# Residual added on VectorE, norms in SBUF, a shared column multiplication and six output buffers in the combine stage of a two-layer mixture-of-experts trunk

## The chip, the cores and the metric

The kernel runs on one core of a Trainium2 chip. The metric is the device time in microseconds (us) of one execution, as the median of several. The program's engines are TensorE (PE, its weight loads PEld), VectorE (DVE), ScalarE (ACT), GpSimd (POOL) and SyncE (SP, which here only issues transfers).

## The reference

Two layers work on 1024 tokens of 1024 columns, all in float32. Each layer has a mixer and then a mixture of experts, in which every token goes to two experts. This is what ends a layer; the change touches nothing else:

```python
y = hierarchical_moe(h, ...)                      # for each token: w0 * expert row 0 + w1 * expert row 1
x = layer_norm(DEEPNORM_ALPHA * x + (1.0 + gt_f) * y, ln_ffn_g[layer], ln_ffn_b[layer])
# layer_norm: (x - mean) * rsqrt(var + eps) * g + b, over the 1024 columns of a token
```

## The kernel before

The program is a row of stages, each with an instruction list of its own for every engine, written out by hand; the lists of a stage start when the engines have left the stage before. The experts' stage writes two scaled rows for each token to memory (`y_dram`). The last stage of each layer, `combine`, then brings them together. It is the stage that changes, and it runs twice: with the tag `f0c` after layer 0's experts (some 1545 to 1617 us of the span) and with `f1c` after layer 1's (3273 to the end).

`combine` works on eight tiles of 128 tokens, t = 0 to 7. For a tile SP loads the two sets of expert rows (`r0`, `r1`) and the residual `x`, 512 KB each, in four buffers. TensorE forms the sum in PSUM (`py`, three buffers): in each half of 512 columns two matmuls with a diagonal matrix of the tokens' weights (L2759) and one with ALPHA times the identity on `x` (L2760), each recorded as two passes. VectorE takes mean and variance from PSUM (`bn_stats` L2782, `bn_aggr` L2784), and adds epsilon (L2786). ScalarE takes the root (L2809), VectorE the reciprocal (L2791) and `nmr` = -mean * rstd (L2793), both of one column. ScalarE normalizes from PSUM into `z` in SBUF (L2817, four buffers), VectorE multiplies by the gain row (L2800), GpSimd adds the bias row (L2827) and issues the store (L2829).

VectorE's list is a loop over n in which three tiles are under way: statistics of tile n, then reciprocal and `nmr` of tile n-1, then the gain of tile n-2. In `f0c` the next layer's input is prepared as well: TensorE transposes each finished tile (L322, after the bias of that tile), and ScalarE (L328) and VectorE (L335) bring the halves to SBUF with a scale and a shift; VectorE does that for tile n-3 at the end of round n. In `f0c` SP also issues the first loads of the next stage's weights (`ret_w`) behind its last `x`.

The waits that matter: TensorE waits for all three loads of a tile and, from tile 3, for the normalization of tile t-3. The gain waits for ScalarE's normalization, the bias for the gain, and the store for the bias. `f1c` ends with the last store, `f0c` with the last tile's L335.

Of the kernel before, what the change touches and what calls it, by code (L numbers as in the profile page):

```python
# [17 lines left out]
P = 128  # L18
D = 1024
# [2693 lines left out]
def combine(g, tag, r, y_dram, x_dram, out_dram, layer, ahead=None):  # L2713
    nc, io = g.nc, g.io
    NR, NB = 4, 3
    with ExitStack() as ctx:  # L2716
# [11 lines left out]
        names = "vec_in weighed summed stat moments rooted rstdd nmrd normed gained done".split()  # L2728
        S = dict(zip(names, g.sems(ctx, tag, *names)))
        r_in = g.sems(ctx, tag, *[f"r_in{b}" for b in range(NR)])  # L2730
        stored = g.sems(ctx, tag, *[f"stored{b}" for b in range(NR)])
        block = g.stage(ctx)

        @block.sync
        def _(sp):
            for t in range(NT):
                if t >= NR:
                    sp.wait_ge(S["summed"], t - NR + 1)
                for k in range(2):
                    sp.dma_start(rows[k][t % NR][:, :], y_dram[k * T + t * P:k * T + (t + 1) * P, :])\  # L2740
                        .then_inc(r_in[t % NR], 16)
                sp.dma_start(x[t % NR][:, :], x_dram[t * P:(t + 1) * P, :]).then_inc(r_in[t % NR], 16)
                if t == 1:
                    sp.dma_start(gain_b[:, :], io["ln_ffn_g"][layer].partition_broadcast(P)).then_inc(S["vec_in"], 16)
                    sp.dma_start(bias_b[:, :], io["ln_ffn_b"][layer].partition_broadcast(P)).then_inc(S["vec_in"], 16)
            if ahead:
                ahead.first_loads(sp)

        @block.tensor
        def _(pe):  # L2750
            pe.wait_ge(S["weighed"], 2 * NT + 1)
# [53 lines left out]
        def _(act):  # L2805
            for n in range(NT + 3):
# [121 lines left out]
```

## Time and profile before

| what | value |
|---|---|
| median of 3 executions | 3352.03 us (3344.8, 3352.03, 3352.76) |
| the profiled execution's own time | 3342.8 us |
| its span, first to last instruction | 3341.1 us |
| TensorE busy | 3009.4 us, 90% of the span |
| VectorE / ScalarE / GpSimd busy | 1211.8 / 879.7 / 582.9 us |
| stage `f0c`, first VectorE instruction to last | 1545.66 to 1616.32 us |
| stage `f1c`, first VectorE instruction to the last store's issue | 3273.30 to 3336.74 us |
| memory traffic in the span | 606.22 MB read, 45.40 MB written |

Times of the table's lower part are microseconds from the span's start. The share of busy time is an average over all stages, and the two combine stages are some 72 and 68 us of 3341; so they are to be read for themselves. The profiled execution is 9 us below the median of the others.

### The profile page before, as it was taken

To read this page: it belongs to the slowest core of one execution; us is meant where nothing else is said; L and a number is where in the kernel's file an instruction comes from. 1 tells how busy PE (TensorE), PEld (TensorE's weight loads), DVE (VectorE), ACT (ScalarE), POOL (GpSimd) and SP (SyncE) were. 2 spreads that over 40 slices of the span, in tenths; PEclk is the share of its full clock that TensorE was granted. 3 is DMA by queue.
4 is the path that set the end of the run, shared out by engine and by line. 5 is a ranking of instruction groups with operands and counts; after the bars stand their busy time and mean duration, and the time that the engine had idled before them with its cause. 6 is when DMAs were issued, how large, how long until landed. Compare 5 with 4: busy or idle time off the path is not lost. (4 is left out here: it accounts for less than half of the span.)

```text
span 3341.1 us, 45315 instructions
## 1 busy us (share of the span) xinstructions
PE 3009.4 (90%) x16595; PEld 1617.1 (48%) x16596; DVE 1211.8 (36%) x3016; ACT 879.7 (26%) x1770; POOL 582.9 (17%) x1031
## 2 busy tenths in 40 slices
PE   8969999698969999998899999999899969988886
PEld 6546544485434443333566666666544434433332
DVE  5867844473442122223333223322312231221224
ACT  1034334142121111111354445544501111111111
POOL 0000010471111222212211111111200011221213
PEclk9979999698979999999899999999999979999998
DMA  8910011233168999996311101110041088999985
GB/s 328 351 55 1 1 29 48 62 75 106 66 261 338 401 419 417 414 404 234 129 38 38 33 6 39 38 38 1 1 147 38 32 350 349 375 423 410 420 359 217
DMA packets 181866, 625.66 MB, mean 187 GB/s; under 512 B 53795, under 2 KB 104754, under 8 KB 147670
## 3 DMA queue, kind: packets, MB, share of 16 engines
q1 hardware_dynamic: 152150, 579.05, 44.4%
q0 software_dynamic: 20576, 42.01, 3.3%
q10 hardware_dynamic: 8992, 2.62, 0.3%
q8 instruction: 93, 1.52, 0.2%
q14 instruction: 55, 0.45, 0.0%
HBM read 606.22 MB, written 45.40 MB: 195 GB/s over the span
## 5 line engine op out<-in xcount | busy, mean ns | idle before, releaser
L1977 PE MATMUL ret_pqkv<-ret_w,hT_mix 128*128 128x512 f32 x1024 | 452.4, 595 | 1.9 <-PEq L2716 1.9
L1839 PE MATMUL mo_py<-mo_w,mixT 128*128 128x512 f32 x768 | 336.2, 598 | 4.8 <-DMA mo_w<-in_ret_w_out_dram 2.5
L2530 PE MATMUL f1e_pgu<-f1w_gu,f1e_xT 128*64 128x512 f32 x1056 | 253.3, 635 | 65.6 <-DMA f1w_gu<-in_moe_w_up_dram 53.5
L1977 PEld LDWEIGHTS ret_pqkv<-ret_w,hT_mix 128*128 128x128 f32 x1024 | 190.5, 191 | 218.0 <-issue 218.0
L2530 PE MATMUL f0e_pgu<-f0w_gu,f0e_xT 128*64 128x512 f32 x1056 | 247.9, 624 | 32.5 <-DMA f0w_gu<-in_moe_w_up_dram 15.0
L1839 PEld LDWEIGHTS mo_py<-mo_w,mixT 128*128 128x128 f32 x768 | 146.4, 192 | 187.4 <-issue 179.5
L1985 PE MATMUL ret_pgate<-ret_w,hT_mix 128*128 128x256 f32 x1024 | 231.6, 379 | 0.0
L1985 PEld LDWEIGHTS ret_pgate<-ret_w,hT_mix 128*128 128x128 f32 x1024 | 189.6, 190 | 23.6 <-issue 0.5
L2530 PEld LDWEIGHTS f1e_pgu<-f1w_gu,f1e_xT 128*64 128x64 f32 x1056 | 82.9, 146 | 228.3 <-issue 171.9
L2127 DVE TENSOR_TENSOR ret_state<-ret_state,ret_pout 128x256 f32<-128x256 f32 x56 | 23.6, 421 | 441.3 <-PE ret_pout L2009 441.3
L2530 PEld LDWEIGHTS f0e_pgu<-f0w_gu,f0e_xT 128*64 128x64 f32 x1056 | 82.8, 144 | 187.6 <-issue 168.6
L478 PE MATMUL gc_pq<-hT_mix,gc_w 128*128 128x512 f32 x384 | 168.3, 597 | 0.7 <-PEq L861 0.7
L1963 POOL TENSOR_TENSOR ret_z<-ret_z,ret_gain 128x256 f32<-128x256 f32 x64 | 46.5, 726 | 653.2 <-DVE ret_z L2138 653.2
L2680 DVE COPY f1e_hidT<-f1e_ph 128x384 f32<-128x384 f32 x33 | 18.4, 558 | 336.8 <-PE f1e_ph L2554 336.7
L2680 DVE COPY f0e_hidT<-f0e_ph 128x384 f32<-128x384 f32 x33 | 18.4, 558 | 331.6 <-PE f0e_ph L2554 331.6
L2562 PE MATMUL f1e_pd<-f1w_d,f1e_hidT 128*64 128x512 f32 x528 | 120.6, 598 | 1.1 <-DVE f1e_hidT L2680 1.1
L2562 PE MATMUL f0e_pd<-f0w_d,f0e_hidT 128*64 128x512 f32 x528 | 120.6, 598 | 0.9 <-DVE f0e_hidT L2680 0.9
L2641 ACT ACTIVATE f1e_hs<-f1e_pgu 128x256 f32<-128x256 f32 x33 | 12.7, 384 | 411.2 <-PE f1e_pgu L2530 411.2
L2048 ACT COPY ret_v<-ret_pqkv 128x256 f32<-128x256 f32 x64 | 23.8, 373 | 368.0 <-PE ret_pqkv L1977 368.0
L478 PEld LDWEIGHTS gc_pq<-hT_mix,gc_w 128*128 128x128 f32 x384 | 73.4, 192 | 92.9 <-issue 92.9
L2641 ACT ACTIVATE f0e_hs<-f0e_pgu 128x256 f32<-128x256 f32 x33 | 12.7, 384 | 384.0 <-PE f0e_pgu L2530 384.0
L1699 DVE TENSOR_TENSOR mo_z<-mo_py,mo_gate_b 128x1024 f32<-128x1024 f32 x16 | 19.6, 1225 | 238.2 <-PE mo_py L1839 238.2
(591 smaller groups left out, 4719.4 us busy)
## 6 DMA issues: line engine op xcount, KB each, us to landing
f0w_gu<-in_moe_w_gate_dram SPq DMA_DIRECT2D x33, 2048.0 KB, 18.4
f0w_gu<-in_moe_w_up_dram SPq DMA_DIRECT2D x33, 2048.0 KB, 26.4
f0w_d<-in_moe_w_down_dram SPq DMA_DIRECT2D x66, 1024.0 KB, 19.5
f1w_gu<-in_moe_w_gate_dram SPq DMA_DIRECT2D x33, 2048.0 KB, 20.0
f1w_gu<-in_moe_w_up_dram SPq DMA_DIRECT2D x33, 2048.0 KB, 30.8
f1w_d<-in_moe_w_down_dram SPq DMA_DIRECT2D x66, 1024.0 KB, 22.0
mixT<-in_ada_w_dram SPq DMA_DIRECT2D x80, 512.0 KB, 5.9
ret_w<-in_ret_w_in_dram SPq DMA_DIRECT2D x16, 1024.0 KB, 10.0
```

What stands on the lines that cost most here:

```text
L478: mm = pe.matmul(pq[u][:, half * 512:(half + 1) * 512], w[u][:, kk, :], g.hT[:, kk, half * 512:(half + 1) * 512], start=(kk == 0), stop=(k ...
L1699: dve.tensor_tensor(z[:, :], y, self.gate_b[:, :], ALU.mult).then_inc(S["zmul"], 1)
L1839: mm = pe.matmul(py[t % 3][:, half * 512:(half + 1) * 512], mixT[:, kk, t * P:(t + 1) * P], ws[:, kk, half * 512:(half + 1) * 512], start= ...
L1963: pool.tensor_tensor(zb, zb, gain[:, h, :], ALU.mult).then_inc(S["gained"], 1)
L1977: mm = pe.matmul(p_qkv[s % 2][:, :], g.hT[:, kk, t * P:(t + 1) * P], w[h % 2][:, kk, 0:512], start=(kk == 0), stop=(kk == KD - 1))
L1985: mm = pe.matmul(p_gate[s % 2][:, 0:RDV], g.hT[:, kk, t * P:(t + 1) * P], w[h % 2][:, kk, 512:W], start=(kk == 0), stop=(kk == KD - 1))
L2048: act.copy(v[b][:, :], p_qkv[s % 2][:, QK:512])
L2127: ch.mark(dve.tensor_tensor(st[:, :], state[(s - 1) % 2][:, :], p_out[:, RDV:2 * RDV], ALU.add))
L2530: mm = pe.matmul(pgu[0][h * LOW:(h + 1) * LOW, :], xT[u][:, kk, 0:LOW], ew.gu[u][:, :, kk, h * FH:(h + 1) * FH], start=(kk == 0), stop=(kk ...
L2562: mm = pe.matmul(pd[0][h * LOW:(h + 1) * LOW, :], hidT_low[:, k % 2, k // 2, :], ew.d[u][:, k, h * DH:(h + 1) * DH], start=(k == 0), stop= ...
L2641: act.activation(hs[0][:, :], pgu[0][:, 0:FH], ACT.Silu).then_inc(S["silu_a"], 1)
L2680: dve.tensor_copy(hidT[:, :], ph[:, 0:4 * CAP]).then_inc(S["hTd"], 1)
```

## The change

TensorE no longer adds the residual: the matmuls with ALPHA times the identity go. VectorE adds ALPHA * x as it takes the sum from PSUM into `z`, and statistics, normalization, gain and bias all work in SBUF. A PSUM buffer is free once VectorE has taken the sum, and TensorE waits for two of the weight matrices and for the expert rows only. `x` has semaphores of its own. The gain is split: VectorE multiplies columns 0 to 511, GpSimd columns 512 to 1023, and then GpSimd adds the bias to all. On VectorE the gain now stands ahead of the reciprocal and `nmr` in a round. `z` has six buffers.

```diff
-    NR, NB = 4, 3
+    NR, NB, NZ = 4, 3, 6
+    HD = D // 2
...
-                sp.dma_start(x[t % NR][:, :], x_dram[t * P:(t + 1) * P, :]).then_inc(r_in[t % NR], 16)
+                if t >= NR:
+                    sp.wait_ge(S["residual"], t - NR + 1)
+                sp.dma_start(x[t % NR][:, :], x_dram[t * P:(t + 1) * P, :]).then_inc(x_in[t % NR], 16)
...
-            pe.wait_ge(S["weighed"], 2 * NT + 1)
             for t in range(NT):
-                pe.wait_ge(r_in[t % NR], 48 * (t // NR + 1))
+                pe.wait_ge(S["weighed"], 2 * t + 2)
+                pe.wait_ge(r_in[t % NR], 32 * (t // NR + 1))
                 if t >= NB:
-                    pe.wait_ge(S["normed"], t - NB + 1)
+                    pe.wait_ge(S["residual"], t - NB + 1)
...
-                        pe.matmul(py[t % NB][:, cols], weights[:, t, k, :], rows[k][t % NR][:, cols], start=(k == 0), stop=False)
-                    mm = pe.matmul(py[t % NB][:, cols], alpha[:, :], x[t % NR][:, cols], start=False, stop=True)
+                        mm = pe.matmul(py[t % NB][:, cols], weights[:, t, k, :], rows[k][t % NR][:, cols], start=(k == 0),
+                                       stop=(k == 1))
...
                     dve.wait_ge(S["summed"], t + 1)
+                    dve.wait_ge(x_in[t % NR], 16 * (t // NR + 1))
...
+                    dve.scalar_tensor_tensor(out=zt[:, :], in0=x[t % NR][:, :], scalar=ALPHA, in1=py[t % NB][:, :],
+                                             op0=ALU.mult, op1=ALU.add).then_inc(S["residual"], 1)
+                    dve.wait_ge(S["residual"], t + 1)
                     for half in range(2):
-                        dve.bn_stats(stats[:, t, half, :], py[t % NB][:, half * 512:(half + 1) * 512]).then_inc(S["stat"], 1)
+                        dve.bn_stats(stats[:, t, half, :], zt[:, half * HD:(half + 1) * HD]).then_inc(S["stat"], 1)
...
+                if 0 <= n - 2 < NT:
+                    t = n - 2
+                    if t == 0:
+                        dve.wait_ge(S["vec_in"], 32)
+                    dve.wait_ge(S["normed"], t + 1)
+                    dve.tensor_tensor(z[t % NZ][:, 0:HD], z[t % NZ][:, 0:HD], gain_b[:, 0:HD], ALU.mult).then_inc(S["gained_a"], 1)
                 if 0 <= n - 1 < NT:
...
-                if 0 <= n - 2 < NT:
-                    t = n - 2
-                    if t == 0:
-                        dve.wait_ge(S["vec_in"], 32)
-                    dve.wait_ge(S["normed"], t + 1)
-                    dve.tensor_tensor(z[t % NR][:, :], z[t % NR][:, :], gain_b[:, :], ALU.mult).then_inc(S["gained"], 1)
...
-                    act.activation(z[t % NR][:, :], py[t % NB][:, :], ACT.Identity, bias=nmr[:, t:t + 1],
+                    act.activation(z[t % NZ][:, :], z[t % NZ][:, :], ACT.Identity, bias=nmr[:, t:t + 1],
...
-                pool.wait_ge(S["gained"], t + 1)
-                pool.tensor_tensor(z[t % NR][:, :], z[t % NR][:, :], bias_b[:, :], ALU.add).then_inc(S["done"], 1)
+                zt = z[t % NZ]
+                pool.wait_ge(S["normed"], t + 1)
+                pool.tensor_tensor(zt[:, HD:D], zt[:, HD:D], gain_b[:, HD:D], ALU.mult).then_inc(S["gained_b"], 1)
+                pool.wait_ge(S["gained_a"], t + 1)
+                pool.wait_ge(S["gained_b"], t + 1)
+                pool.tensor_tensor(zt[:, :], zt[:, :], bias_b[:, :], ALU.add).then_inc(S["done"], 1)
```

The first place is VectorE's list in `f1c`, the round of tile 4 and the start of the next. A number behind `py`, `z` or `x` is that of the buffer. Before, the round is:

```order
L2782 BN_STATS f1c_stats<-f1c_py1 128x6 x2
L2784 BN_AGGR f1c_mv<-f1c_stats 128x2
L2786 TENSOR_SCALAR f1c_rstd<-f1c_mv 128x1
L2791 RECIPROCAL f1c_rstd<-f1c_rstd 128x1
L2793 SCALAR_TENSOR_TENSOR f1c_nmr<-f1c_mv,f1c_rstd 128x1
L2800 TENSOR_TENSOR f1c_z2<-f1c_z2,f1c_gain_b 128x1024
L2782 BN_STATS f1c_stats<-f1c_py2 128x6 x2
```

With the change it is:

```order
L2788 SCALAR_TENSOR_TENSOR f1c_z4<-f1c_x0,f1c_py1 128x1024
L2792 BN_STATS f1c_stats<-f1c_z4 128x6 x2
L2794 BN_AGGR f1c_mv<-f1c_stats 128x2
L2796 TENSOR_SCALAR f1c_rstd<-f1c_mv 128x1
L2802 TENSOR_TENSOR f1c_z2<-f1c_z2,f1c_gain_b 128x512
L2807 RECIPROCAL f1c_rstd<-f1c_rstd 128x1
L2809 SCALAR_TENSOR_TENSOR f1c_nmr<-f1c_mv,f1c_rstd 128x1
L2788 SCALAR_TENSOR_TENSOR f1c_z5<-f1c_x1,f1c_py2 128x1024
```

A multiplication-and-addition of 1024 columns has come ahead of the statistics, which now read `z`. The gain is half as wide, and it has moved from behind `nmr` to ahead of the reciprocal: behind the gain came the next tile's statistics, and now come the reciprocal and `nmr` of one column.

The second place is GpSimd's list in `f1c`, about tiles 3 to 5 before:

```order
L2827 TENSOR_TENSOR f1c_z3<-f1c_z3,f1c_bias_b 128x1024
L2829 DMA out_0_dram<-f1c_z3 128x1024
L2827 TENSOR_TENSOR f1c_z0<-f1c_z0,f1c_bias_b 128x1024
L2829 DMA out_0_dram<-f1c_z0 128x1024
L2827 TENSOR_TENSOR f1c_z1<-f1c_z1,f1c_bias_b 128x1024
```

and about tiles 2 and 3 with the change:

```order
L2834 TENSOR_TENSOR f1c_z2<-f1c_z2,f1c_gain_b 128x512
L2837 TENSOR_TENSOR f1c_z2<-f1c_z2,f1c_bias_b 128x1024
L2839 DMA out_0_dram<-f1c_z2 128x1024
L2834 TENSOR_TENSOR f1c_z3<-f1c_z3,f1c_gain_b 128x512
L2837 TENSOR_TENSOR f1c_z3<-f1c_z3,f1c_bias_b 128x1024
```

For each tile a multiplication of 512 columns has come ahead of the addition.

## Rows read from the trace of the kernel before

**Rows 1.** The chain that ended last, one step (start, us, what).

```profile
3320.65 1.72 PE f1c_py L2759 x4
```

**Rows 2.** Timeline of one `f1c` tile (start, us, engine, line, operation, shapes, idle before).

```profile
3307.81 1.29 DVE L2782 BATCH_NORM_STATS2 f1c_stats<-f1c_py 128x6 f32<-128x512 f32 x2 [2.02 <-PE f1c_py L2760]
...
3309.39 0.15 DVE L2786 TENSOR_SCALAR f1c_rstd<-f1c_mv 128x1 f32<-128x1 f32 x1
...
3309.72 1.22 DVE L2800 TENSOR_TENSOR f1c_z<-f1c_z,f1c_gain_b 128x1024 f32<-128x1024 f32 x1
...
3309.84 1.21 ACT L2817 ACTIVATE f1c_z<-f1c_py,f1c_nmr,f1c_rstd 128x1024 f32<-128x1024 f32 x1
...
3311.03 2.34 POOL L2827 TENSOR_TENSOR f1c_z<-f1c_z,f1c_bias_b 128x1024 f32<-128x1024 f32 x1 [1.92 <-DVE f1c_z L2800]
...
3313.67 0.57 POOL L2829 DMA_DIRECT2D out_dram<-f1c_z  x1 [0.30 <-POOL f1c_z L2827]
```

**Rows 3.** Timeline of the end of `f1c`.

```profile
3325.17 1.22 DVE L2800 TENSOR_TENSOR f1c_z<-f1c_z,f1c_gain_b 128x1024 f32<-128x1024 f32 x1
...
3326.31 0.15 DVE L2791 RECIPROCAL f1c_rstd<-f1c_rstd 128x1 f32<-128x1 f32 x1
...
3326.48 2.33 POOL L2827 TENSOR_TENSOR f1c_z<-f1c_z,f1c_bias_b 128x1024 f32<-128x1024 f32 x1 [1.95 <-DVE f1c_z L2800]
...
3326.50 2.33 DVE L2793 SCALAR_TENSOR_TENSOR f1c_nmr<-f1c_mv,f1c_rstd 128x1 f32<-128x1 f32 x1
...
3328.75 4.71 DVE L2800 TENSOR_TENSOR f1c_z<-f1c_z,f1c_gain_b 128x1024 f32<-128x1024 f32 x2
...
3336.18 0.56 POOL L2829 DMA_DIRECT2D out_dram<-f1c_z  x1 [0.30 <-POOL f1c_z L2827]
```

**Rows 4.** Timeline of `f0c`, four places.

```profile
1570.20 1.30 DVE L2782 BATCH_NORM_STATS2 f0c_stats<-f0c_py 128x6 f32<-128x512 f32 x2 [3.15 <-PE f0c_py L2760]
...
1600.05 1.04 PE L322 MATMUL f0ct_pt<-ident,f0c_z 128*128 128x128 f32 x8
...
1604.58 0.15 DVE L2791 RECIPROCAL f0c_rstd<-f0c_rstd 128x1 f32<-128x1 f32 x1
...
1614.95 1.37 DVE L335 TENSOR_SCALAR hT_mix<-f0ct_pt,mod 128x128 f32<-128x128 f32 x4 [2.14 <-PE f0ct_pt L322]
```

**Rows 5.** Groups of instructions kept apart by shape (total us, mean ns, idle before).

```profile
L1699 DVE TENSOR_TENSOR mo_z<-mo_py,mo_gate_b 128x1024 f32<-128x1024 f32 x16 | 19.6, 1225 | 238.2 <-PE mo_py L1839 238.2
...
L1492 DVE TENSOR_TENSOR dr_Td<-dr_Td,dr_b 128x512 f32<-128x512 f32 x16 | 10.9, 679 | 4.3 <-PE dr_b L1250 4.3
...
L458 POOL TENSOR_TENSOR gdn_gate<-gdn_gate,gc_onorm 128x512 f32<-128x512 f32 x8 | 9.9, 1263 | 2.7 <-DMA gc_onorm<-in_gdn_norm_dram 2.7
```

**Rows 6.** Timeline, VectorE and GpSimd at once, two places.

```profile
697.74 0.21 POOL L1201 TENSOR_TENSOR dr_X<-dr_X,dr_outer 64x15 f32<-64x15 f32 x1
...
697.75 0.68 DVE L1542 TENSOR_REDUCE dr_oss<-dr_y 128x8 f32<-128x512 f32 x1
...
1652.20 0.73 POOL L1963 TENSOR_TENSOR ret_z<-ret_z,ret_gain 128x256 f32<-128x256 f32 x1 [33.41 <-DVE ret_z L2138]
...
1652.25 0.29 DVE L2119 TENSOR_TENSOR ret_scores<-ret_pscores,upto 128x128 f32<-128x128 f32 x1 [0.20 <-PE ret_pscores L1999]
```

**Rows 7.** The third tile's expert rows, `f1c`, then `f0c`: issues and landing.

```profile
L2740 SPq DMA_DIRECT2D f1c_r<-expert_rows x2: 486/532/579, 3277.2 to 3277.8; - x2
...
DMA to landing us min/median/max: 10.4/10.8/11.2
...
L2740 SPq DMA_DIRECT2D f0c_r<-expert_rows x2: 433/436/438, 1550.5 to 1550.9; - x2
...
DMA to landing us min/median/max: 9.9/10.3/10.7
```

**Rows 8.** Windows with TensorE partly idle (window, us, busy by engine, clock, DMA).

```profile
214.00:235.00 21.00, 16.26 (x46) 8.03 (x44) 18.99 (x78) 2.35 (x4) 0.00 (x0) 1.00 0.00 0
...
2410.00:2434.00 24.00, 12.14 (x22) 6.08 (x23) 4.40 (x16) 7.28 (x12) 4.35 (x6) 0.50 0.41 159
```

More of the change, by code:

```diff
@@ L2720, in combine @@
         rows = [[sb(f"r{k}_{b}", [P, D]) for b in range(NR)] for k in range(2)]
-        z = [sb(f"z{b}", [P, D]) for b in range(NR)]
+        z = [sb(f"z{b}", [P, D]) for b in range(NZ)]
         weights = sb("weights", [P, NT, 2, P])
-        alpha = sb("alpha", [P, P])
         stats = sb("stats", [P, NT, 2, 6])
@@ L2727, in combine @@
         turn = Turn(g, ctx, f"{tag}t", layer + 1, 0) if ahead else None
-        names = "vec_in weighed summed stat moments rooted rstdd nmrd normed gained done".split()
+        names = "vec_in weighed summed residual stat moments rooted rstdd nmrd normed gained_a gained_b done".split()
         S = dict(zip(names, g.sems(ctx, tag, *names)))
         r_in = g.sems(ctx, tag, *[f"r_in{b}" for b in range(NR)])
-        stored = g.sems(ctx, tag, *[f"stored{b}" for b in range(NR)])
+        x_in = g.sems(ctx, tag, *[f"x_in{b}" for b in range(NR)])
+        stored = g.sems(ctx, tag, *[f"stored{b}" for b in range(NZ)])
         block = g.stage(ctx)
@@ L2763, in _ @@
                     pe.wait_ge(S["done"], t - 2)
-                    turn.tensor(pe, t - 3, z[(t - 3) % NR])
+                    turn.tensor(pe, t - 3, z[(t - 3) % NZ])
             if turn:
@@ L2767, in _ @@
                     pe.wait_ge(S["done"], t + 1)
-                    turn.tensor(pe, t, z[t % NR])
+                    turn.tensor(pe, t, z[t % NZ])
         @block.vector
         def _(dve):
-            dve.tensor_scalar(alpha[:, :], g.ident[:, :], ALPHA, None, ALU.mult).then_inc(S["weighed"], 1)
             for t in range(NT):
@@ L2778, in _ @@
                 if n < NT:
-                    t = n
+                    t, zt = n, z[n % NZ]
                     dve.wait_ge(S["summed"], t + 1)
+                    dve.wait_ge(x_in[t % NR], 16 * (t // NR + 1))
+                    if t >= NZ:
+                        dve.wait_ge(stored[t % NZ], 16 * (t // NZ))
+                        if turn:
+                            dve.wait_ge(turn.turned, 2 * (t - NZ + 1))
+                    dve.scalar_tensor_tensor(out=zt[:, :], in0=x[t % NR][:, :], scalar=ALPHA, in1=py[t % NB][:, :],
+                                             op0=ALU.mult, op1=ALU.add).then_inc(S["residual"], 1)
+                    dve.wait_ge(S["residual"], t + 1)
                     for half in range(2):
-                        dve.bn_stats(stats[:, t, half, :], py[t % NB][:, half * 512:(half + 1) * 512]).then_inc(S["stat"], 1)
+                        dve.bn_stats(stats[:, t, half, :], zt[:, half * HD:(half + 1) * HD]).then_inc(S["stat"], 1)
                     dve.wait_ge(S["stat"], 2 * t + 2)
@@ L2825, in _ @@
             for t in range(NT):
-                pool.wait_ge(S["gained"], t + 1)
-                pool.tensor_tensor(z[t % NR][:, :], z[t % NR][:, :], bias_b[:, :], ALU.add).then_inc(S["done"], 1)
+                zt = z[t % NZ]
[4 more added lines that the diff above has]
+                pool.tensor_tensor(zt[:, :], zt[:, :], bias_b[:, :], ALU.add).then_inc(S["done"], 1)
                 pool.wait_ge(S["done"], t + 1)
-                pool.dma_start(out_dram[t * P:(t + 1) * P, :], z[t % NR][:, :]).then_inc(stored[t % NR], 16)
-            for b in range(NR):
-                pool.wait_ge(stored[b], 16 * (NT // NR))
+                pool.dma_start(out_dram[t * P:(t + 1) * P, :], zt[:, :]).then_inc(stored[t % NZ], 16)
+            for b in range(NZ):
+                pool.wait_ge(stored[b], 16 * ((NT - 1 - b) // NZ + 1))
 def moe(g, tag, x_dram, out_dram, layer, logits, router, following=None):
```

6 lines of the change are left out of this document (1 added, 5 removed).

## The prediction

> **What bounds the kernel now.** I read the chain of waits first. In the last stage it runs through TensorE's matmuls from tile to tile; one half of a tile's expert rows is four passes in 1.72 us, so 0.43 us each [rows 1]. A tile has 12 passes before, 5.16 us. The timeline of one tile confirms it: VectorE sat idle for 2.02 us until TensorE's last pass, started the statistics at 3307.81 and was through with the gain at 3310.94 [rows 2]. So `f1c` goes by TensorE up to its last tile; behind that VectorE, ScalarE and GpSimd follow one another, and the last store is issued at 3336.18 [rows 3]. `f0c` is the same with transposes: TensorE needs 5.16 and the eight transposes, recorded as 1.04 with the last one's end, so some 6.0 us a tile, the statistics of tile 2 start at 1570.20, VectorE's list reaches the reciprocal of tile 7 at 1604.58, and its last L335 ends at 1616.32 [rows 4]. Elsewhere nothing is edited. The change can only be worth what these two stages, 140 us, give or take.
>
> The second thing to see is at the end of `f1c`. The gain of tile 5 ends at 3325.17 + 1.22 = 3326.39. GpSimd's bias addition starts 0.09 later, at 3326.48. VectorE's `nmr`, one column wide, starts at 3326.50 and takes 2.33 us, to 3328.83, while the bias addition ends at 3328.81 [rows 3]. So a VectorE instruction with two inputs in SBUF stands still while GpSimd's addition runs. Two instructions elsewhere ran free: one with an input in PSUM took 0.29 us inside a GpSimd multiplication of 0.73, and a reduction of 512 columns from one input in SBUF took 0.68 though a GpSimd operation of 0.21 had begun 0.01 before it [rows 6]; 0.68 is what two-input instructions of that width take alone [rows 5]. Before, this costs little: in the running stage the gain is followed by statistics out of PSUM, and `nmr` comes 3.6 us later.
>
> **The change part by part.** Counted from a round's start on VectorE (the residual of tile n):
>
> *Residual.* New, 1024 columns, one input in PSUM: 1.225 us, the nearest group with such inputs and width [rows 5], and 0.03 to the next. By its inputs it doesn't meet GpSimd [rows 6].
>
> *Statistics to epsilon.* From the first `bn_stats` to the epsilon instruction 3309.39 - 3307.81 = 1.58, and an instruction that waits for nothing starts some 0.07 later [rows 2]. I take the same from SBUF. No row has `bn_stats` on SBUF beside GpSimd; bounds are 0 and a full hold (a rival below). I take 0: of the rows, the one-input reduction from SBUF is nearest, and it wasn't held [rows 6]. That it is the second input which makes an instruction wait is a reading, not shown.
>
> *Half a gain, moved forward.* 0.68 us for 512 columns [rows 5]. It starts at 1.255 + 1.58 + 0.07 = 2.91 and ends at 3.59.
>
> *What now stands behind the gain.* Exactly what stood there at the end of `f1c`: reciprocal, `nmr`. GpSimd's wait for this gain is the same kind of wait as before, and its own half is done by then: normalization of tile n-1 (1.21) starts with its `nmr`, at 0.1 of the next round, ends at 1.3, and GpSimd's half (1.26 [rows 5]) runs from 1.4 to 2.7, 0.9 ahead of the other half's end. So the bias addition starts at 3.59 + 0.09 = 3.68 and holds until 6.01; `nmr` starts at 3.70, loses by 0.02, ends at 6.03, and the next round starts 0.08 before that, at 5.95 (3328.75 against 3328.83 [rows 3]). **A round is 5.95 us where TensorE's tile was 5.16.** Without the hold it would be 3.8.
>
> *TensorE.* Eight passes, 3.44 us. Tile 2's rows land at 3277.8 + 11.2 = 3289.0 in `f1c` and at 1550.9 + 10.7 = 1561.6 in `f0c`, held up by the loads ahead and not by an engine [rows 7]. So VectorE's round 2 starts at 3289.0 + 0.1 + 3.44 = 3292.5 and at 1565.1, 5.0 and 5.1 us sooner than before (3307.81 less two tiles is 3297.5; 1570.20).
>
> *`f1c` in sum.* Five rounds: 3292.5 + 29.8 = 3322.3 starts round 7, against 3307.81 + 3 x 5.16 = 3323.3. Then, from 3322.3: `nmr` of tile 6 at 6.0, normalized 7.3, VectorE's half 8.0, GpSimd's 9.3 (it can't run beside the other), `nmr` of tile 7 beside neither, 9.3, bias of tile 6 to 11.7, VectorE's last half behind it 12.3, store 12.6, GpSimd's half 13.9, bias 16.3, store issued 16.6, that is 3338.9. Before: 3336.2. **+2.7 us.**
>
> *`f0c` in sum.* A round has L335 too, 1.37 [rows 4]: 7.32. 1565.1 + 5.95 + 5 x 7.32 = 1607.7 against 1604.58. The rest, laid out the same way: halves 1.3 and 1.8, bias 4.2, `nmr` 4.3, L335 5.7, halves 6.9 and 7.4, bias of tile 7 to 9.8, transposes at the lower clock (2 x 1.04) and L335: 13.2 against 11.7. It ends at 1620.9 against 1616.3. **+4.6 us.**
>
> *At nothing:* the removed weight matrix and the smaller first waits (tile 2's landing hides them), the six buffers (with four, a buffer would be wanted 4 rounds = 24 us later, long after its store), the waits of `x` on SP: tile 7's load is issued some 3 us sooner than before, and the `ret_w` loads behind it as well; their first user is the next stage. If that cover went, tile 7 would come later by at most the 11 us that a load takes to land [rows 7].
>
> Sum: 7.3 us. The profiled execution's own 3342.8 becomes 3350.1. Its own time lies 9.2 below the median 3352.03, so against the runs shown I forecast 3352.0 + 7.3 = **3359**.
>
> The Trainium skill, SBUF — State Buffer, section on who interferes with whom, says that a VectorE instruction with two SBUF inputs contends with a GpSimd instruction that reads SBUF, that whichever starts first keeps the port for its whole length, and that one with a single SBUF input outside the two-port modes is free. The trace agrees (2.33 us for one column), and by that rule `bn_stats` on SBUF costs nothing extra, which no row shows.
>
> **Rivals.**
> 1. *`nmr` gets in ahead of the bias.* The margin is 0.02 us in one event, and GpSimd now has two waits ahead of its addition. Then GpSimd's own round bounds: 1.26 + 0.07 + 2.34 + 0.30 + 0.57 + 0.09 = 4.63, with 0.25 for a meeting with VectorE 4.9; in `f0c` VectorE's 3.8 + 1.37 + 0.25 = 5.4. `f1c`: 3292.5 + 3.9 + 4 x 4.9 + 16.6 = 3332.6 (-3.6); `f0c`: 1565.1 + 3.9 + 5 x 5.4 + 1.3 for the first transpose + 13.2 = 1610.5 (-5.8). Total -9: 3343. It decides as soon as GpSimd starts 0.03 later. Against it: the second wait is for GpSimd's own half, over 0.9 us before. Chance 0.14.
> 2. *`bn_stats` on SBUF is held by GpSimd's half.* The second one would start at 1.9 and wait to 2.7: +0.65 in 12 rounds, +8: 3367. Chance 0.10.
> 3. *The clock falls.* TensorE's own work is 3.44 of 5.95 us and 4.3 of 7.32, 58%. A stretch with TensorE busy 77% had clock 1.00, one with 51% had 0.50 [rows 8]. At 1.2 GHz a tile costs 6.88, and 6.88 + 2.1 with transposes: +0.9 and +1.7 in five rounds each, +13: 3372. Against it: at 1.2 GHz TensorE's 6.88 us would fill the round, and before the change, where it fills its rounds, its passes stay at 0.43 us [rows 1]. Chance 0.08.
> 4. *No change that shows:* terms cancel. 0.03.
>
> The Trainium skill, TensorE: Matmul & The Clock Gate, on oscillation, warns that waits between bursts throw the clock back to half; this is rival 3, and rows 8 agree in direction.
>
> **How the numbers follow.** My forecast has 0.65; its own range is 3351 to 3366. Over all, 3343 takes in rival 1 and 3370 rival 2; what is left out is rival 3 and an error of the sum. A measurement tells 0.3%, 10 us, from no change. The forecast's +7 with some 5 us of doubt is within 0.3% in two cases of three, else slower: 0.42 same, 0.21 slower, 0.02 faster. Rival 1: 0.06 faster, 0.08 same. Rivals 2 and 3: 0.15 slower, 0.03 same. With rival 4: faster 0.08, same 0.56, slower 0.36.
>
> **What would show it.** `nmr` (L2809) in rounds 2 to 7 at 2.3 us beside the bias addition (L2837); if it is 0.16, rival 1 holds. Rounds of 5.95 and 7.3 us between residuals. Residual 1.22, `bn_stats` 0.69 each (more is rival 2). VectorE's round 2 five us sooner. TensorE's clock at 1.00 in both stages' middle (0.50 is rival 3). Wrong altogether would be a third tile that lands later, or work elsewhere that moves.

## The result and the profile after

| | executions | median us | range |
|---|---|---|---|
| before | 20 | 3346.34 | 3339.44 to 3353.05 |
| with the change | 20 | 3356.17 | 3348.87 to 3368.05 |

The ratio is 1.0028, 95% interval 1.0020 to 1.0036, so the changed kernel is slower by 9.4 us (6.7 to 12). 7.3 us were forecast. The profiled execution of the changed kernel has a span of 3348.1 us, 7.0 above the one of before.

The timeline of one `f1c` round of the changed kernel, VectorE's and GpSimd's rows (start, us, engine, line, operation, shapes, idle before):

```profile
3311.63 0.68 DVE L2802 TENSOR_TENSOR f1c_z<-f1c_z,f1c_gain_b 128x512 f32<-128x512 f32 x1
...
3312.23 0.15 DVE L2807 RECIPROCAL f1c_rstd<-f1c_rstd 128x1 f32<-128x1 f32 x1
...
3312.39 2.34 POOL L2837 TENSOR_TENSOR f1c_z<-f1c_z,f1c_bias_b 128x1024 f32<-128x1024 f32 x1 [0.94 <-DVE f1c_z L2802]
...
3312.42 2.33 DVE L2809 SCALAR_TENSOR_TENSOR f1c_nmr<-f1c_mv,f1c_rstd 128x1 f32<-128x1 f32 x1
...
3314.66 1.21 DVE L2788 SCALAR_TENSOR_TENSOR f1c_z<-f1c_x,f1c_py 128x1024 f32<-128x1024 f32 x1
...
3315.02 0.59 POOL L2839 DMA_DIRECT2D out_dram<-f1c_z  x1 [0.30 <-POOL f1c_z L2837]
...
3315.91 1.29 DVE L2792 BATCH_NORM_STATS2 f1c_stats<-f1c_z 128x6 f32<-128x512 f32 x2
...
3316.10 1.26 POOL L2834 TENSOR_TENSOR f1c_z<-f1c_z,f1c_gain_b 128x512 f32<-128x512 f32 x1 [0.49 <-ACT f1c_z L2823]
...
3317.54 0.68 DVE L2802 TENSOR_TENSOR f1c_z<-f1c_z,f1c_gain_b 128x512 f32<-128x512 f32 x1
```

What [rows 3] showed once, at the end of `f1c`, now stands in every running round. VectorE's half gain ends at 3312.31, GpSimd's bias addition starts at 3312.39, `nmr` (one column) at 3312.42, and it ends with the addition. The next residual starts at 3314.66. From gain to gain it is 5.91 us. The statistics run from 3315.91 on and GpSimd's own half of the gain from 3316.10 to 3317.36, and neither waits for the other.

The groups kept apart by shape (total us, mean ns, idle before) say the same of all eight tiles:

```profile
L2809 DVE SCALAR_TENSOR_TENSOR f1c_nmr<-f1c_mv,f1c_rstd 128x1 f32<-128x1 f32 x8 | 15.2, 1894 | 0.3
...
L2792 DVE BATCH_NORM_STATS2 f1c_stats<-f1c_z 128x6 f32<-128x512 f32 x16 | 10.3, 685 | 0.3
...
L2788 DVE SCALAR_TENSOR_TENSOR f1c_z<-f1c_x,f1c_py 128x1024 f32<-128x1024 f32 x8 | 9.7, 1212 | 11.3 <-PE f1c_py L2762 11.3
```

`nmr` took 0.16 us on the first tile, 2.33 on six and 1.03 on the last. `bn_stats` from SBUF takes 0.685 us, the residual 1.212; their sizes were forecast as 0.69 and 1.225.

The timeline, VectorE's residual of tiles 2 and 7 and the last store's issue in `f1c`:

```profile
3296.88 1.22 DVE L2788 SCALAR_TENSOR_TENSOR f1c_z<-f1c_x,f1c_py 128x1024 f32<-128x1024 f32 x1 [3.41 <-PE f1c_py L2762]
...
3326.49 1.21 DVE L2788 SCALAR_TENSOR_TENSOR f1c_z<-f1c_x,f1c_py 128x1024 f32<-128x1024 f32 x1
...
3343.04 0.58 POOL L2839 DMA_DIRECT2D out_dram<-f1c_z  x1 [0.30 <-POOL f1c_z L2837]
```

Five rounds take 29.61 us, 5.92 each, and from the start of round 7 to the last issue it is 16.55 us. In `f0c` the residual of tile 2, the first instruction of round 8, and the last L335, which answer to [rows 4]:

```profile
1563.36 1.22 DVE L2788 SCALAR_TENSOR_TENSOR f0c_z<-f0c_x,f0c_py 128x1024 f32<-128x1024 f32 x1 [2.06 <-PE f0c_py L2762]
...
1605.93 0.69 DVE L2802 TENSOR_TENSOR f0c_z<-f0c_z,f0c_gain_b 128x512 f32<-128x512 f32 x1
...
1617.04 1.37 DVE L335 TENSOR_SCALAR hT_mix<-f0ct_pt,mod 128x128 f32<-128x128 f32 x4 [3.12 <-PE f0ct_pt L322]
```

From the residual of tile 2 to round 8 are 42.57 us, and 12.48 from there to the end.

TensorE's transposes and next tile in `f0c`, the residual that waits for them, then two windows (us, busy by engine, clock, DMA):

```profile
1578.12 1.94 PE L322 MATMUL f0ct_pt<-ident,f0c_z 128*128 128x128 f32 x8 [4.17 <-ACT hT_mix L328]
...
1579.85 4.34 PE L2762 MATMUL f0c_py<-f0c_r,f0c_weights 128*128 128x512 f32 x8
...
1584.23 1.22 DVE L2788 SCALAR_TENSOR_TENSOR f0c_z<-f0c_x,f0c_py 128x1024 f32<-128x1024 f32 x1 [0.45 <-PE f0c_py L2762]
...
1575.00:1580.00 5.00, 1.88 (x9) 1.91 (x10) 4.90 (x12) 2.84 (x6) 2.14 (x3) 0.79 1.02 413
...
3299.00:3310.00 11.00, 9.95 (x23) 3.69 (x21) 10.72 (x16) 2.78 (x4) 7.19 (x5) 1.00 1.03 411
```

TensorE had been idle for 4.17 us. Its eight transposes then took 1.94 us where those of the other four tiles of the running rounds took 1.06 to 1.09, the clock of the window is 0.79, a mixture of the two levels (1.2 and 2.4 GHz), and VectorE waited 0.45 us. The transposes of the last three tiles, at the stage's end, took 1.94 to 1.97 us as well. In the middle of `f1c` the clock stays at 1.00.

### The profile page after: what moved, and what is told of

Its sections match the earlier page's. It is cut to its first block and busy times, and to the rows that moved or that the text cites. A ratio compares the mean times of both kernels' runs of the same rounds, so it can differ in the third digit from the quotient of the medians.

```text
span 3348.1 us, 45251 instructions
## 1 busy us (share of the span) xinstructions
PE 2982.4 (89%) x16531; PEld 1600.4 (48%) x16532; DVE 1244.2 (37%) x3030; ACT 880.2 (26%) x1770; POOL 602.9 (18%) x1047
```

## Experiments

Times were taken against the kernel before on the same chip. Behind each ratio stands its 95% interval. The table has one profiled execution of each kernel: the length of `f0c` (VectorE's first instruction to the end of its last L335) and of `f1c` (VectorE's first instruction to the end of the last store's issue), as differences from the kernel before, which has 70.7 and 63.4 us. What the landing of the first loads and TensorE's clock do ahead of tile 2 moves these by up to 3 us.

| kernel | ratio | `f0c` | `f1c` |
|---|---|---|---|
| with the change | 1.0028 (1.0020 to 1.0036) | +4.9 | +4.1 |
| half gain behind `nmr` | 0.9988 (0.9979 to 0.9997) | +0.7 | 0.0 |
| `nmr` with one tensor input | 0.9994 (0.9985 to 1.0003) | -4.1 | -0.5 |
| before, gain ahead of `nmr` | 1.0038 (1.0025 to 1.0052) | +7.3 | +8.5 |
| whole gain on VectorE, ahead | 1.0031 (1.0019 to 1.0043) | +7.5 | +4.1 |
| whole gain on VectorE, behind | 0.9982 (0.9972 to 0.9993) | +0.5 | -6.5 |
| the same, ScalarE stores | 0.9979 (0.9969 to 0.9989) | -3.6 | -6.0 |
| the same, VectorE's tail, GpSimd stores | 0.9972 (0.9962 to 0.9982) | -1.7 | -8.1 |
| VectorE's tail and ScalarE stores | 0.9967 (0.9957 to 0.9978) | -1.5 | -8.2 |
| with the change, four `z` buffers | 1.0028 (1.0018 to 1.0038) | +6.0 | +6.2 |
| before, gain shared | 1.0008 (0.9998 to 1.0019) | +1.3 | +2.6 |

### The order alone

The half gain behind `nmr`:

```diff
-                if 0 <= n - 2 < NT:      # wait normed, VectorE's half of the gain
-                    ...
                 if 0 <= n - 1 < NT:      # reciprocal, nmr
                     ...
+                if 0 <= n - 2 < NT:      # wait normed, VectorE's half of the gain
+                    ...
```

> The changed kernel with one edit: VectorE's half of the gain stands behind the reciprocal and nmr again, as before the change. Theory (the held nmr sets the round): nmr takes 0.16 to 0.2 us in every round, because GpSimd's bias addition now starts beside the next residual, which has an input in PSUM; a round of f1c falls from 5.9 to 4.6 us (GpSimd's 1.26 + 2.34 + 0.30 + 0.57 and its gaps), the last store is issued some 3 us sooner than before the change and f0c ends some 5 us sooner: 9 us under the kernel before, ratio 0.997. Rival (the round is long because of the work that VectorE took over, 1.22 us of residual, and the order is indifferent): as the changed kernel, 1.003.

The sign is right and the rival is out: with the order undone the changed kernel is faster than the kernel before, and 0.40% (13 us) faster than with it. The size is not: half of the forecast 9 us. The timeline of one `f1c` round, both engines, says where the rest went:

```profile
3301.81 0.64 POOL L2839 DMA_DIRECT2D out_dram<-f1c_z  x1 [0.30 <-POOL f1c_z L2837]
...
3302.09 1.68 DVE L2803 SCALAR_TENSOR_TENSOR f1c_nmr<-f1c_mv,f1c_rstd 128x1 f32<-128x1 f32 x1
...
3302.46 1.28 POOL L2834 TENSOR_TENSOR f1c_z<-f1c_z,f1c_gain_b 128x512 f32<-128x512 f32 x1
...
3303.69 0.68 DVE L2810 TENSOR_TENSOR f1c_z<-f1c_z,f1c_gain_b 128x512 f32<-128x512 f32 x1
...
3304.45 2.36 POOL L2837 TENSOR_TENSOR f1c_z<-f1c_z,f1c_bias_b 128x1024 f32<-128x1024 f32 x1 [0.71 <-DVE f1c_z L2810]
```

`nmr` is held here too, for 1.68 us. It begins within the issue of a store and ends with GpSimd's own half of the gain, which by its record begins 0.37 us after it. VectorE's half follows, GpSimd waits for it, and a round is 5.24 us where 4.6 were expected. The hold has changed its cause, from the bias addition to the shared multiplication. So it is in five rounds of `f1c`; in `f0c` it shows in full in one round only (1.73 us), and what `f0c` lost instead is told with the whole gain below.

The other way about, the kernel before with the order of the change:

```diff
+                if 0 <= n - 2 < NT:      # the whole gain, moved here
+                    ...
                 if 0 <= n - 1 < NT:      # reciprocal, nmr
                     ...
-                if 0 <= n - 2 < NT:
-                    ...
```

> The kernel before with the order of the change alone: the whole gain stands ahead of the reciprocal and nmr; sums, statistics and normalization from PSUM, GpSimd adds the bias only. Theory: nmr is held for 2.3 us in each round though nothing else is changed; normalization comes later, and with it the PSUM buffer that TensorE waits for: f1c some 5 us longer, f0c some 8, together +12, ratio 1.0037. Rival (the order costs nothing without the residual on VectorE, since TensorE's 5.16 us cover it): ratio 1.000.

Ratio 1.0038 against an expected 1.0037. The group of `nmr` in `f1c`, and a row of TensorE's timeline:

```profile
L2799 DVE SCALAR_TENSOR_TENSOR f1c_nmr<-f1c_mv,f1c_rstd 128x1 f32<-128x1 f32 x8 | 14.3, 1789 | 0.3
...
3318.70 1.96 PE L2759 MATMUL f1c_py<-f1c_r,f1c_weights 128*128 128x512 f32 x4 [1.58 <-ACT f1c_z L2817]
```

`nmr` takes 1.79 us on the mean (2.33 on six tiles), and TensorE, which was never idle in this stretch before, waits 1.58 us for the normalization. So both directions give the same price for the order, some 13 us. (Of the +8.5 of `f1c` in the table 2.3 lie ahead of tile 2's statistics and are no part of it.)

### What makes VectorE wait

```diff
-                    dve.scalar_tensor_tensor(out=nmr[:, t:t + 1], in0=mv[:, t, 0:1], scalar=-1.0, in1=root,
-                                             op0=ALU.mult, op1=ALU.mult)
+                    dve.tensor_scalar(nmr[:, t:t + 1], mv[:, t, 0:1], root, -1.0, ALU.mult, ALU.mult)
```

> The changed kernel with one edit: nmr is computed by a tensor_scalar with one tensor input (the mean) and rstd as its per-partition scalar, in place of the scalar_tensor_tensor with two tensor inputs. Order as in the changed kernel. Theory (a second tensor input in SBUF is what makes VectorE stand still beside GpSimd): nmr 0.16 to 0.2 us, rounds of 4.6 to 4.9 us, ratio 0.997 as with the gain moved behind. Rival (any VectorE instruction of that kind that reads SBUF is held by GpSimd's addition): nmr stays at 2.3 us, rounds 5.9, ratio 1.003.

Two groups of `f1c`. Then the issue of a store, one gain of VectorE and the GpSimd instruction beside it, and the bias addition and the residual that follow:

```profile
L2809 DVE TENSOR_SCALAR f1c_nmr<-f1c_mv,f1c_rstd 128x1 f32<-128x1 f32 x8 | 1.7, 214 | 0.3
...
L2802 DVE TENSOR_TENSOR f1c_z<-f1c_z,f1c_gain_b 128x512 f32<-128x512 f32 x8 | 13.1, 1638 | 2.6 <-ACT f1c_z L2823 2.6
...
3303.35 0.60 POOL L2839 DMA_DIRECT2D out_dram<-f1c_z  x1 [0.31 <-POOL f1c_z L2837]
...
3303.72 2.09 DVE L2802 TENSOR_TENSOR f1c_z<-f1c_z,f1c_gain_b 128x512 f32<-128x512 f32 x1
...
3303.97 1.28 POOL L2834 TENSOR_TENSOR f1c_z<-f1c_z,f1c_gain_b 128x512 f32<-128x512 f32 x1
...
3305.88 2.37 POOL L2837 TENSOR_TENSOR f1c_z<-f1c_z,f1c_bias_b 128x1024 f32<-128x1024 f32 x1 [0.64 <-DVE f1c_z L2802]
...
3306.04 1.21 DVE L2788 SCALAR_TENSOR_TENSOR f1c_z<-f1c_x,f1c_py 128x1024 f32<-128x1024 f32 x1
```

`nmr` with one tensor input took 0.21 us in all 16 cases and was never held, in the place where it had been held for 2.33 us. The Trainium skill, SBUF — State Buffer, section on who interferes with whom, says that a VectorE instruction with at most one SBUF input, outside the two-port modes, doesn't contend with GpSimd; the 0.21 us agree if the per-partition scalar (`rstd`, which lies in SBUF too) isn't counted as an input. The run changed the kind of instruction along with the inputs, but the kind is not what counts: the residual, of the same kind as the held `nmr` but with its second tensor in PSUM, began 0.16 us inside a bias addition of 2.37 us and took its usual 1.21. So the second tensor input in SBUF is shown to be the condition, for this instruction. But the ratio is 0.9994 and not 0.997: now VectorE's half of the gain, with its two inputs, is held in `f1c` (mean 1.64 us in place of 0.68), until GpSimd's half is through, although by the records it began 0.25 us ahead of that. Two instructions that exclude each other stand in the place of one. Rival 1 of the prediction was priced at -9 us with only 0.25 us a round for such meetings.

```diff
-                    dve.tensor_tensor(z[t % NZ][:, 0:HD], z[t % NZ][:, 0:HD], gain_b[:, 0:HD], ALU.mult)
+                    dve.tensor_tensor(z[t % NZ][:, :], z[t % NZ][:, :], gain_b[:, :], ALU.mult)
...
-                pool.tensor_tensor(zt[:, HD:D], zt[:, HD:D], gain_b[:, HD:D], ALU.mult)
```

> The changed kernel without the sharing: VectorE multiplies all 1024 columns, GpSimd adds the bias only; the order is that of the changed kernel. Theory: the hold stays and is preceded by a gain of 1.22 in place of 0.68, so a round is 5.95 + 0.54 = 6.5 us and, in f0c, 7.9: f1c +5, f0c +8 against the kernel before, ratio 1.004. Rival (GpSimd's own work sets the round, the hold lies beside it): GpSimd loses 1.3 us a tile, VectorE's list is 4.4 us, faster than before, 0.997.

1.0031 against 1.004 expected, and the rival's 0.997 is out. Beside the changed kernel's 1.0028 it also says that, with this order, the sharing makes no difference that shows. The run holds the test of who comes first. GpSimd's first two additions of `f1c` and the `nmr` beside each:

```profile
3305.83 0.16 DVE L2809 SCALAR_TENSOR_TENSOR f1c_nmr<-f1c_mv,f1c_rstd 128x1 f32<-128x1 f32 x1
...
3305.88 2.36 POOL L2834 TENSOR_TENSOR f1c_z<-f1c_z,f1c_bias_b 128x1024 f32<-128x1024 f32 x1 [25.99 <-DVE f1c_z L2802]
...
3310.10 2.34 POOL L2834 TENSOR_TENSOR f1c_z<-f1c_z,f1c_bias_b 128x1024 f32<-128x1024 f32 x1 [0.95 <-DVE f1c_z L2802]
...
3310.12 2.34 DVE L2809 SCALAR_TENSOR_TENSOR f1c_nmr<-f1c_mv,f1c_rstd 128x1 f32<-128x1 f32 x1
```

Where `nmr` starts 0.05 us ahead of the addition it takes 0.16 us. Where it starts 0.02 behind, 2.34. The first addition starts 0.16 us behind the end of its gain, the second 0.08. The same pattern stands in both stages of this run and of the one before it with the whole gain ahead (the kernel before, reordered): GpSimd's first addition of a stage starts 0.15 or 0.16 us behind its gain and `nmr` is free, four times of four; each of the 24 later ones with an `nmr` beside it starts 0.08 or 0.09 behind and holds it. So the margin of 0.02 us on which the prediction laid rival 1 is real: here 0.07 us decide over 2.2. In the changed kernel GpSimd's first instruction of a stage is its half of the gain; there the first addition starts 0.08 us behind VectorE's half too, and all 12 are ahead of `nmr` by 0.02 or 0.03. Why the first one of a stage is later was not looked into.

### The whole gain behind `nmr`, and the store's issue

Both edits above together: whole gain on VectorE, behind `nmr`, nothing but the bias and the stores on GpSimd.

> The changed kernel with the whole gain on VectorE, behind the reciprocal and nmr; GpSimd adds the bias and issues the stores. Theory (a VectorE instruction with two inputs in SBUF waits while GpSimd adds or multiplies, and while it issues a store): the bias addition lies beside the next residual and the statistics, and nmr comes at some 2.9 us of the round, in the 0.6 us of the store's issue that begins at 2.7: nmr takes 0.4 to 0.6 us in place of 0.16. A round of f1c is 4.6 us; f1c ends some 5 us and f0c 4 to 5 us sooner than before the change, ratio 0.997. Rival (an issue does not hold the port; what held nmr in the run with the half gain behind was the multiplication alone): nmr 0.16 us, a round 4.4 us, ratio nearly the same.

0.9982, 6 us under the kernel before; 9 to 10 were expected. The issue of a store, `nmr` and gain in one `f1c` round, then a window of `f0c`:

```profile
3305.34 0.58 POOL L2836 DMA_DIRECT2D out_dram<-f1c_z  x1 [0.31 <-POOL f1c_z L2834]
...
3305.58 0.16 DVE L2803 SCALAR_TENSOR_TENSOR f1c_nmr<-f1c_mv,f1c_rstd 128x1 f32<-128x1 f32 x1
...
3305.66 1.22 DVE L2810 TENSOR_TENSOR f1c_z<-f1c_z,f1c_gain_b 128x1024 f32<-128x1024 f32 x1
...
1575.00:1583.00 8.00, 7.58 (x21) 4.41 (x22) 3.65 (x11) 2.84 (x6) 3.90 (x4) 0.62 1.02 409
```

The theory's part on the issue fell: `nmr` begins 0.24 us into the issue and takes 0.16, and the gain begins within it and takes 1.22. A round is 4.29 us, and `f1c` is 6.5 us shorter. What is missing is in `f0c`: TensorE was idle for 3.54 us ahead of the first transposes, ran them in 1.97 and the next tile in 5.54 us, the window's clock is 0.62, and VectorE waited 3.96 us for that tile. The same happened in `f0c` with the half gain behind (a tile in 5.73 us, VectorE idle for 3.42), and where it did not, with the one-input `nmr`, `f0c` is 4.1 us shorter. Tile 2 of `f0c` ran partly at the lower clock too (0.69 from 1563.0 to 1568.5): its residual comes 5.4 us after TensorE began the tile, against 3.7 with the one-input `nmr`. TensorE also began it 0.9 us later after the stage's start than in that run, since the rows landed later. So most, not all, of the missing time goes with the clock. That rests on these traces, one of each kernel; no run forced it.

In the run with the half gain behind, `nmr` began 0.24 to 0.28 us into the issue and was held in five rounds of `f1c`. Only what stands behind the issue differs. That was tried with an instruction that nobody needs:

```diff
                 pool.dma_start(out_dram[t * P:(t + 1) * P, :], zt[:, :]).then_inc(stored[t % NZ], 16)
+                pool.tensor_tensor(spare[:, :], gain_b[:, 0:HD], bias_b[:, 0:HD], ALU.mult).then_inc(S["gained_b"], 1)
+                pool.wait_ge(S["gained_b"], t + 1)
```

> As the run with the whole gain behind nmr, and GpSimd has one more instruction behind the issue of each store: a multiplication of 512 columns (gain times bias into a spare tile, used by nobody), which waits for nothing. It is added work, for the trace alone. In the run without it nmr begins 0.24 us after the start of a store's issue and takes 0.16 us. Theory (a GpSimd instruction that is ready keeps VectorE's two-input instructions out from the issue ahead of it on, before its own recorded start): nmr is held from its place in the issue to the end of the multiplication, 1.6 to 1.7 us, and a round grows from 4.3 to 5.3 us or more. Rival (only a GpSimd instruction that has itself begun holds VectorE): nmr takes 0.16 us, the gain follows it at once, and the multiplication waits for the gain.

One execution, 3352.3 us. Two rounds of `f1c`, each with the issue, `nmr` and the added multiplication:

```profile
3308.86 0.61 POOL L2837 DMA_DIRECT2D out_dram<-f1c_z  x1 [0.30 <-POOL f1c_z L2835]
...
3309.03 1.77 DVE L2804 SCALAR_TENSOR_TENSOR f1c_nmr<-f1c_mv,f1c_rstd 128x1 f32<-128x1 f32 x1
...
3309.49 1.28 POOL L2838 TENSOR_TENSOR f1c_spare<-f1c_gain_b,f1c_bias_b 128x512 f32<-128x512 f32 x1
...
3320.60 0.59 POOL L2837 DMA_DIRECT2D out_dram<-f1c_z  x1 [0.30 <-POOL f1c_z L2835]
...
3320.79 0.16 DVE L2804 SCALAR_TENSOR_TENSOR f1c_nmr<-f1c_mv,f1c_rstd 128x1 f32<-128x1 f32 x1
...
3321.21 2.01 POOL L2838 TENSOR_TENSOR f1c_spare<-f1c_gain_b,f1c_bias_b 128x512 f32<-128x512 f32 x1
```

In the first, `nmr` begins 0.17 us after the issue and 0.46 us ahead of the multiplication's record, and is held to its end. So it was in three rounds of the two stages (1.74 to 1.78 us), at 0.17 or 0.18 us after the issue's start. In the second, `nmr` begins 0.19 us after the issue did, and takes 0.16: here the multiplication waited for the gain, as the rival has it. A GpSimd instruction that is ready behind an issue thus can keep VectorE out before its own record begins, and "whichever starts first keeps the port", on which the prediction drew, doesn't hold by the recorded starts. When it does is open. The distance from the issue alone doesn't tell: 0.19 us was free here, and 0.24 to 0.28 was held with the half gain behind.

ScalarE issues the stores, three tiles back in its list:

```diff
+                if n >= 3:
+                    act.wait_ge(S["done"], n - 2)
+                    act.dma_start(out_dram[...], z[(n - 3) % NZ][:, :]).then_inc(stored[(n - 3) % NZ], 16)
...
-                pool.dma_start(out_dram[t * P:(t + 1) * P, :], zt[:, :]).then_inc(stored[t % NZ], 16)
```

> As the run with the whole gain behind nmr, but ScalarE issues the stores, three tiles back in its own list; GpSimd only adds the bias. Theory: with no issue on GpSimd nmr takes 0.16 us in every running round, a round of f1c is 4.4 us, and the total is 1 to 2 us under that run. Rival (issues do not matter): nmr as in that run, whatever it is there.

0.9979, inside the interval of the run without it. In the running rounds `nmr` is 0.16 us in both, and a round of `f1c` is 4.28. As the issues held nothing, there was nothing to take away: the rival is right. The 4.1 us by which `f0c` is shorter in the one profiled execution are no gain of the edit: 3.0 of them lie ahead of tile 2's residual.

### The ends of the stages, sharing, buffers

```diff
+                    if t >= VT:          # VT = 6 in f0c, 5 in f1c
+                        dve.wait_ge(S["gained_a"], t + 1)
+                        dve.wait_ge(S["done"], t)
+                        dve.tensor_tensor(z[t % NZ][:, :], z[t % NZ][:, :], bias_b[:, :], ALU.add).then_inc(S["done"], 1)
...
-                pool.wait_ge(S["gained_a"], t + 1)
-                pool.tensor_tensor(zt[:, :], zt[:, :], bias_b[:, :], ALU.add).then_inc(S["done"], 1)
+                if t < VT:
+                    ...
```

> As the run with the whole gain behind nmr, and in the end of each stage VectorE also adds the bias (tiles 5 to 7 in f1c, 6 and 7 in f0c), 1.22 us in place of GpSimd's 2.34 and without a hold in between. Theory: f1c ends 4 to 5 us sooner than in that run, f0c about 1 us (the transposes follow there): some 15 us under the kernel before, ratio 0.9955. Rival (VectorE is the bound at the end, so what it takes over costs there what GpSimd saves): as the run with the whole gain behind, 0.997.

0.9972, 9 to 10 us under the kernel before. 15 were expected (0.9955), outside the interval, and the ratio itself doesn't tell this run from the rival's 0.997; the trace of `f1c` does. The bias of tile 5 and of tile 7 on VectorE, and the last store's issue:

```profile
3318.18 1.22 DVE L2815 TENSOR_TENSOR f1c_z<-f1c_z,f1c_bias_b 128x1024 f32<-128x1024 f32 x1
...
3323.24 1.22 DVE L2815 TENSOR_TENSOR f1c_z<-f1c_z,f1c_bias_b 128x1024 f32<-128x1024 f32 x1
...
3324.75 0.53 POOL L2842 DMA_DIRECT2D out_dram<-f1c_z  x1 [1.86 <-DVE f1c_z L2815]
```

From the start of the last residual (3313.78) to the end of the last issue are 11.5 us; with the whole gain behind it was 14.7, with the change 17.1. So the step brought 3.2 of the 4 to 5 us expected in `f1c`. The last `nmr` is no longer held (0.16 us, 2.33 without the step). Part of the gain is missing again in `f0c`, with tiles at 5.1 and 5.3 us on TensorE, partly at the lower clock.

> The whole gain behind nmr on VectorE, the bias of the last tiles on VectorE (tiles 5 to 7 in f1c, 6 and 7 in f0c), and the stores issued by ScalarE: the two edits that were faster each by itself. Theory: in the running rounds nothing changes, since nmr was not held by the issues; at the end ScalarE's issue (0.35 us) is shorter than GpSimd's (0.55), but its list has the issue behind the normalization of later tiles: within 1 us of the run with VectorE's tail, ratio 0.997. Rival (the two gains add): 0.9965.

0.9967, the fastest kernel here, 10 to 11 us under the kernel before and 20 under the changed one. It does not stand apart from the run before it by more than their intervals.

The shared multiplication alone, in the kernel before:

```diff
-                    dve.tensor_tensor(z[t % NR][:, :], z[t % NR][:, :], gain_b[:, :], ALU.mult)
+                    dve.tensor_tensor(z[t % NR][:, 0:512], z[t % NR][:, 0:512], gain_b[:, 0:512], ALU.mult)
...
+                pool.wait_ge(S["normed"], t + 1)
+                pool.tensor_tensor(z[t % NR][:, 512:D], z[t % NR][:, 512:D], gain_b[:, 512:D], ALU.mult)
```

> The kernel before with the shared multiplication alone: VectorE multiplies columns 0 to 511, GpSimd 512 to 1023 and then adds the bias; order, sums and residual as before the change. Theory: in the running rounds TensorE's 5.16 us cover GpSimd's 4.6; at the end of each stage, where tiles 6 and 7 go through GpSimd one behind the other, its 1.26 + 0.1 a tile take the place of the 0.54 that VectorE saves: f1c +2 us, f0c +2 us, ratio 1.001. Rival (the split is a gain, as two engines halve the time of the multiplication): 0.999 or less.

1.0008 with an interval that holds 1.000; the profiled execution has +1.3 and +2.6. Two `nmr` rows near the end of `f1c`:

```profile
3331.60 0.66 DVE L2793 SCALAR_TENSOR_TENSOR f1c_nmr<-f1c_mv,f1c_rstd 128x1 f32<-128x1 f32 x1
...
3332.97 2.33 DVE L2793 SCALAR_TENSOR_TENSOR f1c_nmr<-f1c_mv,f1c_rstd 128x1 f32<-128x1 f32 x1
```

In the running rounds `nmr` is held a little longer each time by GpSimd's half, up to 0.66 us, under TensorE's cover. The expectation agrees, but an effect of this size is not clear of zero, in either direction.

Four `z` buffers in place of six (`NR, NB, NZ = 4, 3, 4`):

> The changed kernel with four z buffers in place of six. Expected: a buffer is written again 4 rounds of 5.9 us after its residual and some 2 us after its store is issued and done, so nothing waits: ratio as the changed kernel, 1.003, residuals start without idle time from round 3 on. Rival (the store is not through in time, and the residual waits for it): rounds from tile 4 on are up to 1 us longer, 1.005.

The ratio is that of the changed kernel, but the trace is not. The store of tile 0 and the residual that takes its buffer again:

```profile
3302.63 0.64 POOL L2839 DMA_DIRECT2D out_dram<-f1c_z  x1 [0.30 <-POOL f1c_z L2837]
...
3311.10 1.22 DVE L2788 SCALAR_TENSOR_TENSOR f1c_z<-f1c_x,f1c_py 128x1024 f32<-128x1024 f32 x1 [2.85 <-DMA out_dram<-f1c_z]
```

The store, issued at 3302.63 beside the loads, landed only 8.4 us later, and the residual waited 2.85 us for it. In `f0c` the same wait was 0.2 us. So the six buffers are worth up to 3 us in `f1c`, which the ratio can't tell. The +6.0 of `f0c` is not theirs: its last running round took 9.03 us, with TensorE's transposes ahead of it at 1.94 us.

## Why the prediction was right

1. *The bound, and where the change can act.* Right. The two stages differ by +4.9 and +4.1 us, the rest of the spans by -2.0. The forecast time of 3359 stands on the median of three executions, 3352.03, and 20 executions put the kernel before at 3346.34. So the time rests on a base 5.7 us too high and a change some 2 us too small, and that these partly cancel is luck. From 3346.34 the forecast 7.3 us give 3353.6 for a measured 3356.17, which is no worse; both figures lie within the range of 3351 to 3366.
2. *The hold sets the round.* Right, in place, order and size: 2.33 us in each of six rounds of both stages, a round of 5.92 us in `f1c` for a forecast of 5.95, and in `f0c` 7.2 for 7.32. The order moved by itself costs 13 us in either kernel. The forecast rested on one row of before with a margin of 0.02 us; the runs with the whole gain ahead show both outcomes. (The prediction puts `nmr` 3.6 us behind the gain in the kernel before; its rows give 3.9, and nothing hangs on it.)
3. *Residual, statistics.* Right. Statistics from SBUF are not held beside GpSimd, so rival 2 is out. A guess of the prediction, that the second input in SBUF decides, is shown for `nmr`, where that input is a tensor.
4. *A start 5 us sooner.* Too large. From the stage's first VectorE instruction, the residual of tile 2 comes 3.4 us sooner than the statistics did in `f1c` and 4.1 in `f0c`. The sum took the landing times of before; with the change tile 2 is run by TensorE from 17.1 us after the start of `f1c`, not 15.7. This is the 1.4 us by which `f1c` came out above its +2.7. In `f0c` the 1.0 us is partly given back at the end, 12.5 us for 13.2.
5. *Six buffers at nothing.* Wrong by up to 2.9 us in the one trace of four buffers: the cover taken, a store that ends long before, is not there while the loads run. It changed nothing in the sum, since the change has the six.
6. *Sharing.* The sum had it as part of a stage's end. By itself it measured 1.0008, which is not clear of zero, and no gain shows.
7. *Rival 1* had the right margin and a wrong price: with `nmr` out of the bias addition's way, GpSimd's half of the gain holds VectorE for 1.4 to 1.5 us a round of `f1c`, where 0.25 was allowed, and the result is some -2 to -4 us, not -9 (the -2 is not clear of zero). It was not the case that came, so the time is untouched.
8. *Rival 3.* In the running rounds the clock did fall once in `f0c`, for one tile, at a cost of 0.45 us, and not in `f1c`. At the end of `f0c` the transposes ran at the lower clock, as the sum had it. In two faster variants VectorE waited 3.4 and 4.0 us for a tile that TensorE ran at the lower clock.

So the change brings three things together: the residual on VectorE with norms in SBUF (and with it the six buffers and the new waits, which weren't tried apart), worth some 6 us by the run with the whole gain behind (0.9982); the sharing, which loses some 2 by the difference from that run (0.9988), less than their intervals can tell from nothing; and the new order, which loses 13.

## What to carry to other kernels

Where VectorE and GpSimd work side by side, look at which instruction follows the one that releases GpSimd. Here a one-column instruction with two tensor inputs in SBUF, 0.16 us long, cost as much as the GpSimd addition that started 0.02 us ahead of it (2.33 us). With the residual, which reads PSUM, in that place, or with `nmr` in a form with one tensor input, nothing was held by the addition. A multiplication shared between these two engines, with both inputs in SBUF, was no halving: their parts took turns, and no run was faster for it beyond its interval. And when one engine is relieved, look at what holds the stage next, landing times and TensorE's clock here.

## What the runs showed of the hardware that was not expected

- A GpSimd instruction that is ready behind the issue of a store can hold a two-input VectorE instruction that begins up to 0.46 us ahead of it by the records (1.68 us with the half gain behind, 1.77 with the added multiplication; once, 0.42 us ahead, it did not). With nothing ready behind the issue, `nmr` and gain run within it unhindered (0.16 and 1.22 us).
- In the kernels whose GpSimd does nothing but add the bias and at most issue stores, its first addition of a stage started 0.15 or 0.16 us behind the gain that released it, and the later ones 0.07 to 0.09. With the whole gain ahead of `nmr`, `nmr` was free beside the first (4 of 4) and held for 2.33 us beside the later ones (24 of 24).
- A store of 512 KB that takes 2.9 us to land in quiet took 8.4 us beside the loads.
- The length of TensorE's idle time alone did not tell at which clock it came back. In `f0c` of the changed kernel the transposes took 1.94 us (1.2 GHz) after 4.17 us of idle time and 1.06 (2.4 GHz) after 3.22; with the half gain behind they took 1.97 after 2.94, and the next tile 5.7 us in place of 3.6. In `f1c` of the changed kernel, after 1.1 to 3.0 us, the clock did not fall; with the half gain behind it did after 2.1 us (a tile in 5.4 us).
